# A lookup that serves 64 tokens with two picks each, its rows summed in two 64-column groups of TensorE

## What is computed

```python
s1, i1 = lax.top_k(sc[:, :, 0], 16); s2, i2 = lax.top_k(sc[:, :, 1], 16)   # per token, per head (8 heads)
top_s, pos = lax.top_k(all 256 sums s1 + s2, 16)      # 16 picks of a head
gate = softmax(top_s)
u = take(u_tab, eidx); act = gelu(einsum('thkd,td->thk', u, x))
vv = take(v_tab, eidx); out = einsum('thk,thkd->td', gate * act, vv)
```

## Times and profile before

| | us |
|---|---|
| median of three runs | 2682.74 |
| lowest and highest | 2680.59, 2694.96 |
| the profiled execution, its own time | 2686.64 |
| its span, first to last instruction | 2684.8 |
| TensorE busy | 2230.6 (83%) |
| VectorE busy | 1793.1 (67%) |
| ScalarE busy | 600.2 (22%) |
| GpSimd busy | 789.9 (29%) |
| HBM read | 959.12 MB, 358 GB/s over the span |

### The profile page before, as it was taken

The page is one execution under the profiler, slowest core; times in us unless marked ns, Lnnn a source line. Parts: engine busy times, 40 slices in busy tenths (PEclk is TensorE's granted clock), DMA queues, the critical chain, the costliest instruction groups (busy, mean ns, idle before and its releaser), DMA issues.

```text
span 2684.8 us, 23465 instructions
## 1 busy us (share of the span) xinstructions
PE 2230.6 (83%) x6452; PEld 1073.4 (40%) x6452; DVE 1793.1 (67%) x5249; ACT 600.2 (22%) x1836; POOL 789.9 (29%) x773
## 2 busy tenths in 40 slices
PE   6777988897899788778887799888889977777776
PEld 2245434444456333333443244444536533232232
DVE  1334467765676677776666757786677777787775
ACT  1222113322122122222211211332212221121111
POOL 0002222222433233322333322222243333333332
PEclk9978998898999998889999999999999999999999
DMA  9948899777999999979999978776899999999997
GB/s 361 387 183 341 308 343 359 263 257 261 389 408 400 394 413 417 395 288 350 416 416 418 417 276 329 265 272 248 323 418 411 404 421 422 421 407 421 416 415 298
DMA packets 188435, 963.28 MB, mean 359 GB/s; under 512 B 15992, under 2 KB 18424, under 8 KB 89232
## 3 DMA queue, kind: packets, MB, share of 16 engines
q0 software_dynamic: 110592, 805.36, 74.7%
q1 hardware_dynamic: 77712, 156.44, 15.9%
HBM read 959.12 MB, written 2.62 MB: 358 GB/s over the span
## 4 chain that ended last, share of the span: by engine, by line
PE 47%; DMA 22%; DVE 21%; issue 5%; ACT 3%; POOL 1%; SPq 0%; DVEq 0%; POOLq 0%; ACTq 0%
PE ps_acc L904 24%; DMA ring<-peer_uv,rows 17%; DVE ring L1406 8%; PE ps_mm L739 7%; PE ps_mm L886 5%; PE ps_mm L858 3%; DMA ring<-ada_w 2%; PE ps_mm L796 2%; POOL ring L656 1%; DMA weights<-w_in 1%; DMA weights<-peer_wq 1%; DMA weights<-ada_w 1%; PE ps_mb L679 1%; DVE poly L1413 1%; ACT poly L1077 1%
## 5 line engine op out<-in xcount | busy, mean ns | idle before, releaser
L904 PE MATMUL ps_acc<-ring,diags 128*128 128x512 f32 x3072 | 1456.2, 624 | 218.2 <-ACT diags L1084 215.2
L656 POOL DMA_INDIRECT ring<-peer_uv,rows x768 | 787.9, 1026 | 1864.6 <-PE ps_acc L904 1515.5
L904 PEld LDWEIGHTS ps_acc<-ring,diags 128*128 128x128 f32 x3072 | 591.5, 199 | 997.7 <-issue 645.9
L1406 DVE CUSTOM_DVE_ANT_0 ring<-ring,ps_tr 128x1024 f32<-128x1024 f32 x512 | 620.7, 1220 | 193.8 <-DMA ring<-peer_uv,rows 162.9
L1406 DVE CUSTOM_DVE_ANT_0 ring<-ring,h 128x1024 f32<-128x1024 f32 x256 | 310.8, 1223 | 44.9 <-DMA ring<-peer_uv,rows 27.2
L1077 ACT ACTIVATE poly<-poly 128x2 f32<-128x2 f32 x384 | 77.6, 202 | 1163.3 <-DVE poly L1414 1163.1
L1084 ACT ACTIVATE diags<-consts,coef 128x128 f32<-128x128 f32 x768 | 265.5, 393 | 115.9 <-DVE coef L1425 113.7
L1425 DVE SCALAR_TENSOR_TENSOR coef<-poly,gated 128x2 f32<-128x2 f32 x384 | 61.9, 161 | 221.5 <-ACT poly L1077 220.0
L886 PE MATMUL ps_mm<-hT,weights 128*128 128x128 f32 (+1 forms) x1024 | 188.4, 341 | 17.6 <-DMA weights<-peer_wq 9.3
L739 PE MATMUL ps_mm<-weights,hT 128*128 128x512 f32 x432 | 191.7, 597 | 12.3 <-DMA weights<-w_in 11.2
L886 PEld LDWEIGHTS ps_mm<-hT,weights 128*128 128x128 f32 x1024 | 167.9, 203 | 54.6 <-issue 32.9
(11 more groups left out here) (201 smaller groups left out, 1498.4 us busy)
## 6 DMA issues: line engine op xcount, KB each, us to landing
weights<-w_in SPq DMA_DIRECT2D x17, 2048.0 KB, 15.8
weights<-peer_wq SPq DMA_DIRECT2D x16, 2048.0 KB, 18.7
weights<-ada_w SPq DMA_DIRECT2D x14, 2048.0 KB, 13.1
ring<-ada_w SPq DMA_DIRECT2D x10, 2048.0 KB, 16.6
ring<-peer_uv,rows POOLq DMA_INDIRECT x768, 12.0
weights<-w_out SPq DMA_DIRECT2D x6, 2048.0 KB, 21.6
ring<-w_in SPq DMA_DIRECT2D x3, 2048.0 KB, 20.0
ring<-w_out SPq DMA_DIRECT2D x2, 2048.0 KB, 16.2
```

The lines of the kernel that those rows point to most:

```text
L656: pool.indirect_dma_start(ring[:, n % SLOTS, :], None, peer_uv1 if n >= PICKS // 2 else peer_uv0, bass.IndirectOffsetOnAxis(ap=picks, axis ...
L904: last = pe.matmul(ps_acc[:, b * NB:(b + 1) * NB], diags[:, n % DIAGS, :], ring[:, n % SLOTS, DM + b * NB:DM + (b + 1) * NB], start=(i == ...
L1406: dve.tensor_tensor_reduce(row, row, h, 1.0, 0.0, ALU.mult, ALU.add, of_head(dots, n)).then_inc(u_used, 1)
```

## The change

One gather now fetches rows for 64 tokens, with two picks each: step n serves the token half n mod 2; partition p holds the row of token `64 * half + p mod 64`, and the upper 64 partitions hold a pick 8 further on in the same head than the lower 64. What follows from it:

- **Sums.** A group of two steps is the two halves. `add_pair` multiplies a 128x64 matrix (two 64x64 diagonals one above the other) with the slot, so that the two picks of a token are added in the multiplication, and puts the 64 rows into the lower or the upper half of `ps_acc`'s partitions. Half 0 uses columns 0 to 63 of the array, half 1 columns 64 to 127. A group still has eight MATMUL records, each of 64 columns of weights. Both diagonals must be there before the first of them.
- **Normed rows twice.** `h_twice` in SBUF holds for each half its 64 rows on the lower and again on the upper partitions. `hold_rows` writes it with four copies of 64x1024 at the start of every tile, after the last dot of the tile before; all dots read it. `ps_tr` is no longer needed for it, and `tight` and what hangs on it is gone.
- **Picks and gates.** `route` writes to `found`, and ScalarE spreads it to `rows` with four small copies (64x8) a head; the gates, now scaled once for a whole head, are spread in the same way. `gate_scale` comes nine steps earlier than before.
- **Memory.** `h_twice` takes the 8 KB per partition of one slot: `SLOTS` goes from 9 to 8. `diags` are half as wide.

The bytes fetched, the number of gathers, the number of dots, and the order and weights of the dense pieces stay as they were.

```diff
-SLOTS = 9
+SLOTS = 8
+HALF = P // 2
+PER_HALF = TOPK // 2
-        diags = sb("diags", [P, DIAGS, P])
+        diags = sb("diags", [P, DIAGS, HALF])
+        h_twice = sb("h_twice", [P, 2, DM])
-            return 1 if tight(l, tiles) else 2
...
-                    pool.wait_ge(picks_ready, n // TOPK + 1)
+                    pool.wait_ge(picks_ready, (n // TOPK + 1) * 4)
...
-            def add_rows(n):
+            def add_pair(g):
+                n = g * GROUP
...
-                pe.wait_ge(diag_ready, n + 1)
+                pe.wait_ge(diag_ready, n + GROUP)
                 for b in range(2):
-                    last = pe.matmul(ps_acc[:, b * NB:(b + 1) * NB], diags[:, n % DIAGS, :],
-                                     ring[:, n % SLOTS, DM + b * NB:DM + (b + 1) * NB], ...)
-                last.then_inc(v_used, 1)
+                    for j in range(2):
+                        last = pe.matmul(ps_acc[HALF * j:HALF * (j + 1), b * NB:(b + 1) * NB], diags[:, (n + j) % DIAGS, :],
+                                         ring[:, (n + j) % SLOTS, DM + b * NB:DM + (b + 1) * NB],
+                                         ..., tile_position=(0, HALF * j))
+                        if b:
+                            last.then_inc(v_used, 1)
...
             def hold_rows(tau):
-                act.activation(ps_tr[:], h2[:, tau % T, :], ACT.Copy).then_inc(h_held, 1)
+                act.wait_ge(u_used, tau * TILE)
+                for half in range(2):
+                    for q in range(2):
+                        act.activation(h_twice[HALF * q:HALF * (q + 1), half, :],
+                                       h2[HALF * half:HALF * (half + 1), tau % T, :], ACT.Copy).then_inc(h_held, 1)
+            def spread(to, tokens, ready):
+                for half in range(2):
+                    for q in range(2):
+                        act.activation(to[HALF * q:HALF * (q + 1), half:TOPK:2],
+                                       tokens[HALF * half:HALF * (half + 1), q * PER_HALF:(q + 1) * PER_HALF],
+                                       ACT.Copy).then_inc(ready, 1)
...
+                if i % TOPK == 1 and AHEAD <= i // TOPK + 1 < ALL_HEADS:
+                    spread_rows(i // TOPK + 1)
+                if i % TOPK == 9 and i // TOPK + 1 < ALL_HEADS:
+                    spread_gates(i // TOPK + 1)
...
-                h = h2[:, 0, :]
-                if tau in SAMPLES:
-                    h = ps_tr[:]
+                if n % TILE < 2:
+                    dve.wait_ge(h_held, held(n // TILE, half))
...
-                step.after(dve.scalar_tensor_tensor(out=of_head(gated, n, GROUP), in0=a, scalar=gate_inv[...], in1=gates_of(head)[...]))
+                step.after(dve.tensor_tensor(of_head(gated, n, GROUP), a, of_head(gates, n, GROUP), ALU.mult))
...
+                if k == 7 and head + 1 < ALL_HEADS:
+                    gate_scale(head + 1)
```

More of the change, by code:

```diff
@@ L110 @@
 C_PICK = C_PLUS + 3
-N_CONST = C_PICK + ROWS
+C_PAIR = C_PICK + ROWS
+N_CONST = C_PAIR + HALF
 COND_AT, COND_COLS = 5, 5 + QROWS
@@ L397, in tr, with keys_at, scores_at, probs_at @@
             return ps_tr[:, (i % 2) * NB:(i % 2) * NB + n]
[L399 to L413, removed]
+        transposed = ps_tr
+        def keys_at(j):
+            return tr(j)
+        def scores_at(g, n):
+            return mm(g, n)
+        def probs_at(head, n):
+            return tr(head, n)
         def key_scores_at(l, tiles, i, n):
             return tr(i, n) if (l, tiles) == P0 else ps_mb[:, (i % 2) * NB:(i % 2) * NB + n]
-        def conv_up(l, tiles):
-            return ps_mb[:, CW:2 * CW] if tight(l, tiles) else ps_mb[:, NB:NB + CW]
-        def buffers(l, tiles):
-            return 1 if tight(l, tiles) else 2
+        conv_up = ps_mb[:, NB:NB + CW]
         const_loaded = sem("const_loaded")
@@ L521, in group_nth, with held @@
             return (l * 2 + (tiles == S_TILES)) * per + i + 1
-        def held(tau):
-            return tau // T * len(S_TILES) + tau % T
+        def held(tau, half):
+            return tau * 4 + half * 2 + 2
         def slot_nth(l, tiles, i):
@@ L772, in dense_stages @@
                         pe.matmul(ps_mb[:, 0:CW], shift(1 - P), w_.conv_u[:, 0, :], start=False, stop=True)
-                    last = pe.matmul(conv_up(l, tiles), up, w_.conv_u[:, j, :], start=True, stop=(t != 1))
+                    last = pe.matmul(conv_up, up, w_.conv_u[:, j, :], start=True, stop=(t != 1))
                     if t == 1:
-                        last = pe.matmul(conv_up(l, tiles), shift(P - 1), w_.conv_u[:, 1, :],
+                        last = pe.matmul(conv_up, shift(P - 1), w_.conv_u[:, 1, :],
                                          start=False, stop=True)
@@ L828, in dense_stages @@
                     for head in range(HEADS):
-                        if head + 1 < HEADS and not tight(l, tiles):
+                        if head + 1 < HEADS:
                             scores(head + 1)
@@ L832, in dense_stages @@
                             transpose_probs(head - 1)
-                        if head + 1 < HEADS and tight(l, tiles):
-                            scores(head + 1)
                         if head >= 2:
@@ L1100, in _ @@
             side = Beside(programs)
+            for n in range(AHEAD):
+                spread_rows(n)
             gate_exps(0)
+            spread_gates(0)
             for i in range(PICKS):
                 tau, j = i // TILE, i % TILE
-                if j == 0 and tau in SAMPLES and tau - 1 in SAMPLES:
+                if j == 0:
                     hold_rows(tau)
@@ L1114, in _ @@
                     copy_sum(tau - 1)
-                if j == TILE - 2 and tau + 1 in SAMPLES and tau not in SAMPLES:
-                    hold_rows(tau + 1)
             copy_sum(DEPTH * T - 1)
@@ L1399, in dot @@
                 row = ring[:, n % SLOTS, 0:DM]
-                tau = n // TILE
-                h = h2[:, 0, :]
-                if tau in SAMPLES:
-                    h = ps_tr[:]
-                    if n % TILE == 0:
-                        dve.wait_ge(h_held, held(tau))
-                dve.tensor_tensor_reduce(row, row, h, 1.0, 0.0, ALU.mult, ALU.add, of_head(dots, n)).then_inc(u_used, 1)
+                half = n % 2
+                if n % TILE < 2:
+                    dve.wait_ge(h_held, held(n // TILE, half))
+                dve.tensor_tensor_reduce(row, row, h_twice[:, half, :], 1.0, 0.0, ALU.mult, ALU.add, of_head(dots, n)).then_inc(u_used, 1)
             def polynomial(g):
```

79 lines of the change are left out of this document (45 added, 34 removed).

## The result

The changed kernel takes 2653.23 us (median; 2643.83 to 2654.48). The ratio to the kernel before is 0.9873, 95% interval 0.9836 to 0.9911: 34 us faster (24 to 44), where 111 were forecast. The profiled execution takes 2654.05 us, its span is 2652.2.

What follows compares the result with a forecast made beforehand. It took the sums' chain on TensorE to hold the mixer stretches and DMA to limit the lookup-only ones; 132 - 5 - 6 - 10 = 111 us gained, forecast 2572 us, range 2490 to 2660.

Steps and rivals of the forecast that it cites:

- The sums: Whole kernel: two column groups abreast shorten the sums on TensorE, gaining 132 us together before the 10 us for the clock.
- three quarters: Mixer stretches: share of the 58 and 64 us freed on the chain that would be realised, 44 and 48 us.
- two thirds of the wall: Two middle stretches: share of the 18 and 33 us DMA limit that would be gained, 12 and 22 us.
- The wall: All stretches: gain if DMA alone were left at 422 GB/s, 333 us summed, 18 and 33 in the middle ones.
- Rival 1: Mixer stretches bound by VectorE and handing over between engines; one third realised there, 2643 us; chance 0.20.
- Its sign, a chain led by VectorE: Mixer stretches after the change: a chain of waits led by VectorE would show rival 1 right.
- The ring: Gather slots, nine to eight: lost slot hidden by the queue of gathers, 0 us; 170 us without that cover.
- The start of a tile: Copies of normed rows hold VectorE some 4 us, six times; two starts uncovered at 3 us each, 6 us.
- the cover: Four tile starts where DMA is the limit: queue of landed or flying rows hides the copies; 24 us without any.
- ScalarE: Small spreading copies, 22 us in the mixer stretches, less 16 saved by narrower diagonals: net 5 us charged.
- The change of shape: TensorE, both ends of nearly every group of sums: 0.2 us a group, bounds 0 and 0.30.
- The clock: TensorE idles more with shorter sums, so its granted clock falls: 10 us charged.

Runs made afterwards that it cites:

- column groups alone: Changed kernel without copies of normed rows (dots read the tile's rows as they are), without spreading of picks and gates, with nine slots: 2605.0 us, ratio 0.9693.
- half sums: Kernel before with columns 512 to 1023 of the sums left out in all but the first and last step of each tile: 2599.5 us, ratio 0.9681.
- half dots: Kernel before with columns 512 to 1023 left out of every dot product: 2651.2 us, ratio 0.9881; with the sums halved too, 2541.7 us, 0.9458.
- tiny sums: Kernel before with all but 32 columns of the sums left out in all but each tile's first and last step: 2591.4 us, ratio 0.9648.
- without copies: Changed kernel with the copies of normed rows left out, dots reading the tile's rows as they are: 2629.1 us, ratio 0.9782; with nine slots 2613.4 us, 0.9723.
- Split copies: Changed kernel with ScalarE writing half 0 of the normed rows and VectorE half 1: 2640.9 us, ratio 0.9821.
- the second measurement: Spreading of picks and gates left out of the changed kernel that has no copies of normed rows and nine slots: 2605.0 us against 2613.4 us.
- the filler: Changed kernel with one multiplication by zeros added ahead of each group's wait for its diagonals: 2678.3 us, ratio 0.9973; with two, 2726.7 us, 1.0148.

## Why the prediction was wrong

- **The sums, the largest miss: 122 us forecast with the clock, 82 measured by the column groups alone, 86 by half sums.** The length of a group at full clock was right: 1.87 us by the trace against 1.92 forecast. Two groups abreast reached the full 2x, so the row of `modulate` was the better guide. The Trainium skill ("TensorE: Matmul & The Clock Gate", Part 3) has 2.38x for three column tiles; the trace here shows no such loss for two. Two steps failed.

  The first is "three quarters" of the chain in the mixer stretches. Halving L904's part would free 66 and 73 us (half of 132 and 146); half sums brought 35 and 34, a half. The chain gives what one engine has on one path; it can't show the path right behind it. The experiments with half dots show VectorE on that path, and the chain of M2 with half sums is led by it. The clock is the other candidate, below.

  The second is "two thirds of the wall" in mid, 34 us, of which half sums brought 16. Half sums, half dots and tiny sums all end at 792 to 793 us and 403 GB/s there, and the furthest that any run came is 780 us and 409 GB/s. The wall was put at 422 GB/s, which only short windows reach; the share of DMA in the earlier trace rows, 0.99 and 0.95 in the two middle windows, already left only some 385 x 0.01 + 343 x 0.05 = 21 us of the 51 that the rate seemed to leave (18 and 33). In the tail half sums brought nothing, where 6 us were forecast.

  Rival 1 had the first mechanism, with VectorE's 80%, at 20%. Its 2643 us lie near the measured time by luck: it had 61 us from the sums and 21 for all costs, where 82 and some 50 were measured. Its sign, a chain led by VectorE, did not show in the changed kernel, though the dots' part has grown. M1 and M2 of the changed kernel:

```profile
by line: PE ps_acc L904 16.4%; PE ps_mm L739 10.3%; PE ps_mm L884 8.0%; DVE ring L1427 7.5%; DMA weights<-ada_w 6.2%; DMA ring<-peer_uv,rows 5.5%; issue 4.6%; PE ps_mm L856 4.4%; PE ps_mm L796 3.4%; PE ps_mb L698 2.6%; PE ps_mb L822 1.9%; D
by line: PE ps_acc L904 13.8%; PE ps_mm L739 13.3%; DVE ring L1427 11.3%; DMA weights<-peer_wq 6.8%; PE ps_mm L856 6.6%; DMA ring<-peer_uv,rows 4.6%; issue 3.9%; DVE negmax L1278 2.7%; PE ps_mm L796 2.2%; PE ps_mb L679 1.7%; PE ps_mm L884 1
```

- **The ring: 0 forecast, 19 us before the change, 16 in it.** The flight did shrink as argued, from 14.5 to 11.3 us in the tail (the answer to the earlier trace rows for the changed kernel):

```profile
DMA to landing us min/median/max: 6.7/11.3/13.8
```

but a queue that covers the mean did not cover the slot. That the slot is lost at stands of VectorE, where the mean says nothing, would be a guess: eight slots alone cost 5, 6, 4 and 5 us in the four stretches. Between two starts of tiles, from gather 552 to 630, one comes every 2.47 us before and every 2.56 us with eight slots (2.58 in the changed kernel), so a part is lost there too. Why stays open.
- **The start of a tile: 6 us forecast, 24 measured, most of it at the four starts that were put at nothing.** The timelines of ScalarE and VectorE at step 640 of the changed kernel:

```profile
2310.45 4.28 ACT L1091 ACTIVATE h_twice<-h 64x1024 f32<-64x1024 f32 x4
...
2318.05 1.00 ACT L1112 ACTIVATE h<-ps_acc 128x1024 f32<-128x1024 f32 x1
```

```profile
2307.80 1.22 DVE L1427 CUSTOM_DVE_ANT_0 ring<-ring,h_twice 128x1024 f32<-128x1024 f32 x1
...
2312.71 1.23 DVE L1427 CUSTOM_DVE_ANT_0 ring<-ring,h_twice 128x1024 f32<-128x1024 f32 x1 [2.79 <-ACT h_twice L1091]
...
2314.87 1.23 DVE L1427 CUSTOM_DVE_ANT_0 ring<-ring,h_twice 128x1024 f32<-128x1024 f32 x1 [0.92 <-ACT h_twice L1091]
...
2322.92 1.22 DVE L1451 SCALAR_TENSOR_TENSOR h<-h,ps_acc 128x1024 f32<-128x1024 f32 x1 [4.72 <-PE ps_acc L679]
```

The copies hold VectorE for 3.7 us (2.79 + 0.92), as forecast. They also stand on ScalarE in front of the last tile's sum (L1112), and so come before the gate (L679), for which VectorE waits 4.72 us; without copies it waits 3.01 us there. GpSimd shows what comes of it:

```profile
2317.21 1.79 POOL L656 DMA_INDIRECT ring<-peer_uv,rows  x1 [0.30 <-issue]
2328.58 1.96 POOL L656 DMA_INDIRECT ring<-peer_uv,rows  x1 [9.57 <-PE ps_acc L904]
```

No gather starts for 11.4 us, about a flight; without copies the longest such gap is 5.2 us. What failed is the cover: I had priced the copies by themselves, and the end of the old tile, with its sum, its gate and the wait for it, already stood in the same place. That the two share one slack is argued, and only half borne out. Split copies shorten the gap to 9.5 us and the time by 14 us. With the gate out of the way of the sums the gap is 8.3 us and the time no shorter, so the wait for the gate is not what costs by itself.
- **ScalarE: 5 us forecast, 9 measured** for the spreads, the diagonals' saving (53 ns each, against 70) not in it; 8 us by the second measurement. Right in size, within the noise.
- **The change of shape: 0.2 us a group forecast, 0.15 by the trace**; what it costs as a whole is inside the 3 us, within 7, between the column groups alone and half sums. The Trainium skill ("TensorEngine Tiling (Array Packing)", Key Properties) has TensorE drain when the tiling mode changes. The trace agrees in kind, with the 0.15 us.
- **The clock: 10 us forecast.** It fell to 0.84 and 0.88 in the mixer stretches and 0.77 in the tail. In mid and the tail it is not what took the gain: with tiny sums it is 0.56 in the tail and the tail still takes 693 us, and with the clock raised by the filler neither became shorter by more than 2 us. In M1 and M2 its price stays open, and it may be more than 10 us. With half sums TensorE's busy time fell by 73 and 67 us there (442 to 369, 403 to 335), where halving the sums' 210 and 207 should take off 105 and 104: the missing 32 and 36 us are the lower clock's. They are busy time and not time on the chain, and no run tells how much of them lay on it.

The sum as measured: 86 for halved sums, minus 3 for what goes with column groups, minus 16, 24 and 9 for slot, copies and spreads: 34 us, the measured 34. Of the 77 us between forecast and result, some 40 are the sums (122 forecast, 82 measured), 18 the starts of tiles, 16 the slot and 4 the spreads.

## What to carry to other kernels

A line's share of the chain is not what shortening it gives: in the mixer stretches here, with VectorE busy 61 and 68% of them beside TensorE, half of it came. Leaving out half of the second engine's work in an experiment tells what it holds. Where DMA is near its limit, read the room left from its busy share over the stretch, and not from the best rate of a short window. Slack is spent once: before a new stall is put at nothing because a queue covers it, list what already stands in the same place, and try one slot less in the kernel before.

## What the hardware showed

- The gathers take GpSimd longer when the dots of VectorE read both operands from SBUF: 1170 against 948 ns in the same window of two kernels that differ in that and in the copies to PSUM, and within the kernel before 40 and 42 against 4 to 7 gathers a tile over 1.2 us. The Trainium skill ("GPSIMD Engine Reference", Specifications, the row on SBUF interfaces) names contention with VectorE instructions that have two SBUF inputs. The trace agrees. It cost nothing in the kernel before.
- VectorE wrote two of the 64x1024 copies in 1.41 us, where ScalarE takes 1.05 us for one (the version with split copies):

```profile
2299.40 1.41 DVE L1432 COPY h_twice<-h 64x1024 f32<-64x1024 f32 x2
```
- At a lower granted clock TensorE's unchanged work takes longer and need not cost anything: in the tail with tiny sums the clock is 0.56 and the gathers still come at 412 GB/s.
